# First attention of a two-layer hybrid block: second score pass over 64 rows on alternating halves of the array

## The chip, the cores and the metric

The kernel runs on one core of a Trainium2 chip, as one launch. The metric is device time in microseconds: 2327.08 us is the median of three runs (2325.67 to 2328.69). The profiled execution, from which every duration below comes, took 2329.05 us; its span from the first to the last instruction is 2327.2 us. The engines are named as in the profile: PE (TensorE matmul), PEld (its weight loads), DVE (VectorE), ACT (ScalarE), POOL (GpSimd), SP (SyncE).

## The reference, cut to what matters

Two layers over 512 latent tokens and 256 context tokens, width 1024. Each layer has three token mixers in parallel, then a SwiGLU. The change touches mixer A alone, a grouped-query attention: 8 query heads of 64 channels, 2 key/value heads, queries and keys RMS-normalised per head, latents also rotated.

```python
k_all = jnp.concatenate([kac, ka], axis=1)          # context keys, then latent keys
s = jnp.einsum('bqkgd,bskd->bkgqs', q, k).astype(jnp.float32) * (HEAD_DIM ** -0.5)
p = jax.nn.softmax(s, axis=-1).astype(v.dtype)
return jnp.einsum('bkgqs,bskd->bqkgd', p, v)
```

Latent queries see 512 latent and 256 context keys. Context queries see the 256 context keys; they exist in the first layer only, since the last layer has no context output.

## The kernel before, in words

**Numbers in two parts.** The operands of a matmul have type fp32r, which keeps fewer bits than float32. So an array is held as a high part (the value written as fp32r) and a low part (the value minus the high part), and a product is a sum of partial products.

**Queries and keys of the first attention.** For a pair of heads c, `q_st[0][c][x]` is a tile of 128 partitions by 768 tokens for head 2c+x. Its high part has the 64 partitions of half x, its low part the other half. `k_hh[0]` has a key head's high part on both halves, `k_ll[0]` its low part on both halves. One matmul over all 128 rows with `k_hh` gives (high + low) times high key, a second one with `k_ll` gives (high + low) times low key; both add up in PSUM.

**Work items.** Token tiles of 128: 0 to 3 latents, 4 and 5 context. `ORDER[0]` puts them in pairs, whose first member is side 0 and whose second is side 1: (0,1), (3,2) and, in layer 0 alone, (4,5). An item n is a head and a pair, n = head x pairs + j; layer 0 has 24 items, layer 1 has 16. Side 0's scores lie in PSUM banks 0 and 1, side 1's in banks 2 and 3 (`SCORES_AT`). For a latent tile each pass is two matmuls, 512 latent keys and 256 context keys; for a context tile it is one over 256.

**The order on each engine** is written out by hand. PE, in the loop of `attention` for mixer A, item n: `score(n + 1, 0)`, `score(n + 1, 1)`; `turn(n, 0)`, `turn(n, 1)` (transposes of the probabilities, L2292, four to a group); half of a fill (`fill`, L2340: projection work for the gates, put between the attention's steps); `turn(n, 2)`; now and then a `piece` (L2137: transposes that make the queries or keys of a later pair of heads); `attend(n, groups 0 and 1)` (L2310); the other half of the fill; `attend(n, group 2)`. A context pair has one group instead of three. `score` (L2273) does all of side 0, both passes, and then all of side 1; the last matmul of a side raises `scored`. `turn` and `piece` wait until the transposes two before them have been read by DVE (`lo_out`).

**DVE**, item n: `fold(n - 1)` (L1672, after ACT's `o_half` L958, after the last `attend`); `maximum(n + 1, 0)` and `maximum(n + 1, 1)` (L1645, negated by L1648), each after its `scored`; `turned_lo(n, 0)` (L1662, `pt_lo`), `invert(n + 1, 0)` (L1655), `turned_lo(n, 1)`, `invert(n + 1, 1)`, `turned_lo(n, 2)`, then a piece's low part (L1461). **ACT** does the high part of each turned group (L949), the exponentials (L941), and a piece's high part (L884). **POOL** multiplies the probabilities by the inverse sums (L582).

**Pieces of queries.** For either head of a pair ACT copies 64 rows of PSUM to the head's half of `q_st`, and DVE writes the difference to the other half: two instructions on each engine, 512 columns (latents) or 256 (context). There are 12 such pieces: 4 pairs of heads, latents in both layers, context in the first.

Of the kernel before, what the change touches and what calls it, by code (L numbers as in the profile page):

```python
# [5 lines left out]
F32 = mybir.dt.float32  # L6
F32R = mybir.dt.float32r
I32 = mybir.dt.int32
ALU = mybir.AluOpType
ACT = mybir.ActivationFunctionType  # L10
# [4 lines left out]
LAT, CTX = 512, 256  # L15
P = 128
# [3 lines left out]
TOK = LAT + CTX  # L20
HALF = TOK // 2
HD = 64
# [21 lines left out]
ADA_SLOTS = 3  # L44


ORDER = (((0, 1), (3, 2), (4, 5)), ((0, 1), (2, 3), (4, 5)))

FILLS = 8
KEY_COPIES = 2 * 16  # L50
# [3 lines left out]
SCORES_AT = ((0, 1024), (0, 512))  # L54
# [186 lines left out]
def build(nc, x_in, ctx_in, cond, cond_cols, w_first, w_ada, b_ada, stream, qk_gain, norm_rows, bias, ident_in,  # L241
# [8 lines left out]
    def sb(name, shape, dtype=F32, at=None):  # L250
        size = (2 if dtype == mybir.dt.bfloat16 else 4) * int(np.prod(shape[1:]))
        if at is None:
            at = cursor[0]
            cursor[0] += (size + 63) // 64 * 64
        assert at + size <= end, (name, at + size - end)
        return nc.alloc_sbuf_tensor_at(name, shape, dtype, offset=at)
# [57 lines left out]
    q_st = [[[sb(f"q_st{b}{c}{x}", [P, TOK], F32R, at=R + Q_AT[b][c] * K + 3 * K * x) for x in range(2)]  # L314
             for c in range(KB)] for b in range(2)]
    k_hh = [sb(f"k_hh{b}", [P, (2, 4)[b], TOK], F32R, at=R + (87, 42)[b] * K) for b in range(2)]
    k_ll = [sb(f"k_ll{b}", [P, (2, 4)[b], TOK], F32R, at=R + (93, 54)[b] * K) for b in range(2)]
# [35 lines left out]
    ps = nc.alloc_psum_tensor("ps", [P, 8, 512], F32)  # L353
# [55 lines left out]
    def S(name):  # L409
        if name not in sems:  # L410
            sems[name] = nc.alloc_semaphore(name)
        return sems[name]
# [14 lines left out]
    def at(ph, name):  # L427

        return ph.at.get(name, 0) + (PRIME if name in PRIMED else 0)
# [16 lines left out]
    with block:  # L446
# [116 lines left out]
        def _(pool):  # L563
# [9 lines left out]
            def attention(ph):  # L573
                pairs, branch = ph.tiles // 2, ph.part

                def normalise(n, i):

                    j, c = n % pairs, 2 * (n % 2) + i
                    keys = P * len(key_tiles(branch, ORDER[branch][j][i]))
                    pool.wait_ge(S("inverse"), at(ph, "inverse") + 2 * n + i + 1)  # L580
# [51 lines left out]
        def _(act):  # L632
# [240 lines left out]
            def piece(ph, what, h, part):  # L873

                order = turn_order(ph)[what, h, part]
                a, b = ((0, LAT), (LAT, TOK))[part]
                act.wait_ge(S("turned_p"), at(ph, "turned_p") + order + 1)
                for x in range(2):
                    rows = slice(HD * x, HD * x + HD)
                    if what == "q":  # L880
                        dst, src = q_st[0][h][x][rows, a:b], ps[rows, turn_bank(ph, order), 0:b - a]
                    else:
                        dst, src = k_hh[0][rows, h, a:b], ps[HD * h:HD * h + HD, turn_bank(ph, order), 0:b - a]
                    last = nc.scalar.activation(dst, src, ACT.Copy)  # L884
                last.then_inc(S("hi_out"), 1)

# [42 lines left out]
            def attention(ph):  # L929
# [3 lines left out]
                def probs(n, i):  # L933

                    j, c = n % pairs, 2 * (n % 2) + i
                    keys = P * len(key_tiles(branch, ORDER[branch][j][i]))
                    act.wait_ge(S("max_ready"), at(ph, "max_ready") + 2 * n + i + 1)
# [242 lines left out]
        def _(dve):  # L1180
# [268 lines left out]
            def piece(ph, what, h, part):  # L1449

                order = turn_order(ph)[what, h, part]
                a, b = ((0, LAT), (LAT, TOK))[part]
                dve.wait_ge(S("hi_out"), at(ph, "hi_out") + order + 1)
                for x in range(2):
                    rows, other = slice(HD * x, HD * x + HD), slice(HD * (1 - x), HD * (2 - x))
                    if what == "q":
                        src, dst, hi = rows, q_st[0][h][x][other, a:b], q_st[0][h][x][rows, a:b]
                    else:
                        src = slice(HD * h, HD * h + HD)
                        dst, hi = k_ll[0][rows, h, a:b], k_hh[0][src, h, a:b]  # L1460
                    last = nc.vector.tensor_tensor(dst, ps[src, turn_bank(ph, order), 0:b - a], hi.bitcast(F32), ALU.subtract)  # L1461
                last.then_inc(S("lo_out"), 1)

# [157 lines left out]
            def attention(ph):  # L1621
# [3 lines left out]
                def maximum(n, i):  # L1625

                    h, j = divmod(n, pairs)
                    m, t = 2 * n + i, ORDER[branch][j][i]
                    keys = P * len(key_tiles(branch, t))
# [258 lines left out]
        def _(pe):  # L1888
# [356 lines left out]
            def attention(ph):  # L2245
                pairs, branch, turns = ph.tiles // 2, ph.part, turn_order(ph)
                count = HEADS * pairs

                def score(n, i):

                    h, j = divmod(n, pairs)
                    t, m = ORDER[branch][j][i], 2 * n + i
                    if branch == 0 and i == 0 and h % 2 == 0:
                        if j == 0:
                            pe.wait_ge(S("lo_out"), at(ph, "lo_out") + turns["q", h // 2, 0] + 1)
                            if h % 4 == 0:
                                pe.wait_ge(S("lo_out"), at(ph, "lo_out") + turns["k", h // 4, 1] + 1)
                        elif j == 2:
                            pe.wait_ge(S("lo_out"), at(ph, "lo_out") + turns["q", h // 2, 1] + 1)
                    elif branch == 1 and i == 0 and j == 0 and h % 2 == 0:  # L2260
                        pe.wait_ge(S("fill_lo"), at(ph, "fill_lo") + passes_to(ph, h))
                        pe.wait_ge(S("k_dup"), at(ph, "k_dup") + KEY_COPIES * (h // 2))
                    if n:

                        pe.wait_ge(S("probs"), at(ph, "probs") + m - 1)
                    q, kv = q_st[branch][h // 2][h % 2], h // 4 if branch == 0 else h % 4
                    for part, kk in enumerate((k_hh[branch], k_ll[branch])):
                        lat = latent_keys(branch, t)
                        for keys, first, w in ((lat, 0, P * len(lat)), (None, P * len(lat), CTX)):
                            if not w:  # L2270
                                continue
                            at_col = SCORES_AT[branch][i] + first
                            last = nc.tensor.matmul(ps[:, at_col // 512, at_col % 512:at_col % 512 + w], q[:, t * P:(t + 1) * P],  # L2273
                                                    tile_cols(kk[:, kv, :], keys) if keys else kk[:, kv, LAT:TOK],
                                                    start=part == 0 and at_col % 512 == 0, stop=part == 1, skip_group_check=True)
                    last.then_inc(S("scored"), 1)

                def turn(n, g):
# [6 lines left out]
                    for kt in turn_groups(branch, j)[g]:  # L2285
                        for i, t in sorted(enumerate(ORDER[branch][j]), key=lambda e: e[1]):
                            tiles = key_tiles(branch, t)
# [7 lines left out]
                def attend(n, some):  # L2295
# [3 lines left out]
                    for g in some:  # L2299
# [3 lines left out]
                        for x, kt in enumerate(groups[g]):  # L2303
                            v = v_a[:, kt, h // 4, :] if branch == 0 else v_b[:, h // 2, kt, h % 2, :]
                            users = [t for t in ORDER[branch][j] if kt in key_tiles(branch, t)]
                            w, side = P * len(users), P * (min(users, key=lambda t: t % 2) % 2)
# [222 lines left out]
def latent_keys(branch, t):  # L2529

    if t >= LT:
        return ()
    return NEAR_TILES[t] if branch else tuple(range(LT))


def key_tiles(branch, t):

    return latent_keys(branch, t) + tuple(range(LT, ALLT))
# [7 lines left out]
def turn_groups(branch, j):  # L2546

    if j == 2:
        return ((LT, LT + 1),)
    if branch == 0:  # L2550
        return ((LT, LT + 1), (0, 1), (2, 3))
    return ((LT, LT + 1), ((1, 0, 2), (3, 2, 0))[j])
# [8 lines left out]
def tile_cols(cols, tiles):  # L2561

    return cols[:, 0:LAT].rearrange("p (a b) -> p a b", b=P)[:, tiles[0]:tiles[-1] + 1:tiles[-1] - tiles[0] if len(tiles) == 2 else 1, :]
# [19 lines left out]
    return (((1, 0, 4),), ((5, 0, 3), (0, 3, 1)))[j]  # L2583


def start_pieces(ph):

    if ph.part:
        return []
    return [("k", 0, 0), ("q", 0, 0), ("k", 0, 1)] + [("q", 0, 1)] * (ph.tiles > LT)  # L2590
# [14 lines left out]
def turn_bank(ph, order):  # L2605

    return order if order < len(start_pieces(ph)) else TURN_BANK[ph.part] + order % 2


def turn_order(ph):  # L2610

    pairs = ph.tiles // 2
    names = start_pieces(ph) + slot_pieces(ph, -1)
    for n in range(HEADS * pairs):
        names += [("p", n, g) for g in range(len(turn_groups(ph.part, n % pairs)))]
        names += slot_pieces(ph, n)
    return {name: i for i, name in enumerate(names)}
# [19 lines left out]
def passes_to(ph, f):  # L2637

    return sum(len(fill_passes(ph, n)) for n in range(f))
# [195 lines left out]
```

## Time and profile before

| | us |
|---|---|
| median of three runs | 2327.08 |
| profiled execution | 2329.05 |
| its span | 2327.2 |
| PE busy, 97% of the span | 2254.0 |
| DVE busy, 51% | 1187.5 |
| ACT busy, 40% | 929.6 |
| POOL busy, 47% | 1084.1 |

Busy time of PE is not PE at its peak: a matmul's row contains its way through the array, so that rows overlap. The pitch from one start to the next says what a matmul costs in a stream. An idle gap that a row names is therefore shorter than the time that PE loses. The first attention runs from about 262 to 420 us (layer 0) and from about 1533 to 1658 us (layer 1).

### The profile page before, as it was taken

The numbers are of one execution on the slowest core, as the hardware profiler recorded it, in microseconds if no ns is written. First come the engines' busy times: TensorE is split into PE (matmuls) and PEld (weight loads), VectorE is DVE, ScalarE is ACT, GpSimd is POOL, SyncE is SP. The second block draws the span as 40 slices with busy tenths as digits, with TensorE's granted clock in tenths as the row PEclk, the third lists the DMA queues.
The fourth block names the chain that finished last, engine by engine and source line by source line (L and its number), as shares of the span: only waits on it lengthen the run. The fifth ranks groups of instructions, "written<-read, shape, count | busy, mean of one in ns | idle before, by whom it ended". The sixth has DMA issues, their size and how long they took to land.

```text
span 2327.2 us, 34375 instructions
## 1 busy us (share of the span) xinstructions
PE 2254.0 (97%) x13050; PEld 2072.4 (89%) x13050; DVE 1187.5 (51%) x2429; ACT 929.6 (40%) x1854; POOL 1084.1 (47%) x852
## 2 busy tenths in 40 slices
PE   7999999999999999999999989999999999999997
PEld 4899988989999999999999878888889899888887
DVE  5979766527632546654831173656637426212114
ACT  4232466436622651111111254256546447322223
POOL 1334445435534553433533443455545567545545
PEclk9999999999999999999999999999999999999999
DMA  6634200122114445443522433221223256333345
GB/s 267 216 117 131 96 27 24 60 71 82 58 63 136 159 156 187 135 151 117 163 84 66 158 130 128 64 64 37 64 84 98 80 185 189 118 99 100 109 122 176
DMA packets 120083, 266.00 MB, mean 114 GB/s; under 512 B 13701, under 2 KB 13957, under 8 KB 118537
## 3 DMA queue, kind: packets, MB, share of 16 engines
q1 hardware_dynamic: 109728, 238.08, 31.7%
q10 hardware_dynamic: 10216, 26.09, 3.3%
q8 instruction: 85, 1.39, 0.2%
q14 instruction: 54, 0.43, 0.1%
HBM read 250.48 MB, written 10.49 MB: 112 GB/s over the span
## 4 chain that ended last, share of the span: by engine, by line
PE 85%; DVE 8%; ACT 3%; issue 1%; DMA 1%; POOL 1%; ACTq 0%; SPq 0%; DVEq 0%
PE ps L1932 31%; PE ps L1934 13%; PE ps L1944 13%; PE ps L2340 8%; PE ps L2045 7%; PE ps L2310 4%; PE ps L2292 3%; PE ps L2273 2%; PE ps L2119 1%; DVE pt_lo L1662 1%; DVE max_c L1645 1%; DVE ada_unused_gate_up L1192 1%; ACT p_sb L941 1%; DMA raw<-in_stream 1%; PE ps L2000 1%
## 5 line engine op out<-in xcount | busy, mean ns | idle before, releaser
L570 POOL TENSOR_TENSOR w_lo<-raw,w_hi 128x512 fp32r<-128x512 f32 x632 | 864.5, 1390 | 963.8 <-ACT w_hi L648 963.1
L648 ACT ACTIVATE w_hi<-raw 128x512 fp32r<-128x512 f32 x632 | 367.5, 627 | 671.1 <-PE ps L1934 247.1
L1932 PE MATMUL ps<-h_hi,w_lo 128*128 128x384 f32 (+1 forms) x832 | 301.1, 362 | 0.0
L1932 PE MATMUL ps<-h_hi,w_hi 128*128 128x384 f32 (+1 forms) x832 | 300.4, 361 | 0.0
L1932 PE MATMUL ps<-h_lo,w_hi 128*128 128x384 f32 (+1 forms) x832 | 300.4, 361 | 0.0
L582 POOL TENSOR_TENSOR p_sb<-p_sb,row_inv 128x768 f32<-128x768 f32 (+1 forms) x160 | 178.9, 1126 | 197.5 <-DVE row_inv L1655 196.1
L1759 DVE TENSOR_TENSOR ps<-silu_g,ps 128x768 f32<-128x768 f32 (+3 forms) x52 | 37.7, 726 | 377.3 <-PE ps L1934 177.8
L1932 PEld LDWEIGHTS ps<-h_hi,w_lo 128*128 128x128 f32 x832 | 156.2, 188 | 15.8
L1932 PEld LDWEIGHTS ps<-h_lo,w_hi 128*128 128x128 f32 x832 | 156.2, 188 | 15.8
L1932 PEld LDWEIGHTS ps<-h_hi,w_hi 128*128 128x128 f32 x832 | 156.2, 188 | 15.8
L2340 PE MATMUL ps<-h_hi,w_lo 128*128 128x384 f32 (+1 forms) x408 | 147.9, 362 | 3.0 <-DVE v_b L1610 2.3
L1192 DVE SCALAR_TENSOR_TENSOR ada_unused_gate_up<-ada_raw_gate_up,ada_cond_gate_up 128x1024 bf16<-128x1024 f32 x96 | 143.0, 1490 | 5.2 <-DMA ada_raw_gate_up<-in_w_ada 0.2
L2340 PE MATMUL ps<-h_lo,w_hi 128*128 128x384 f32 (+1 forms) x408 | 144.4, 354 | 0.0
L2340 PE MATMUL ps<-h_hi,w_hi 128*128 128x384 f32 (+1 forms) x408 | 144.2, 353 | 0.0
L1934 PE MATMUL ps<-h_hi,w_hi 128*128 128x384 f32 x424 | 141.6, 334 | 0.0
L1934 PE MATMUL ps<-h_hi,w_lo 128*128 128x384 f32 x424 | 141.6, 334 | 0.0
L1934 PE MATMUL ps<-h_lo,w_hi 128*128 128x384 f32 x424 | 141.6, 334 | 0.0
L941 ACT ACTIVATE p_sb<-ps,neg_max 128x768 f32<-128x768 f32 (+1 forms) x160 | 117.0, 731 | 45.6 <-DVE neg_max L1642 36.7
L1662 DVE TENSOR_TENSOR pt_lo<-ps,pt_hi 128x512 fp32r<-128x512 f32 x176 | 118.2, 687 | 30.8 <-ACT pt_hi L949 29.5
L949 ACT ACTIVATE pt_hi<-ps 128x512 fp32r<-128x512 f32 x176 | 101.8, 598 | 63.1 <-PE ps L2292 62.0
L1164 ACT ACTIVATE silu_g<-ps 128x768 f32<-128x768 f32 (+1 forms) x36 | 25.4, 706 | 209.1 <-PE ps L1934 130.5
L2292 PE MATMUL ps<-ident,p_sb 128*128 128x128 f32 x704 | 96.7, 275 | 2.0 <-DVE pt_lo L1662 1.0
(246 smaller groups left out, 5503.4 us busy)
## 6 DMA issues: line engine op xcount, KB each, us to landing
raw<-in_stream SPq DMA_DIRECT2D x632, 256.0 KB, 2.8
ada_raw_gate_up<-in_w_ada SPq DMA_DIRECT2D x48, 512.0 KB, 3.6
ada_raw_tokens_a<-in_w_ada SPq DMA_DIRECT2D x16, 512.0 KB, 3.7
ada_raw_merge_c<-in_w_ada SPq DMA_DIRECT2D x16, 512.0 KB, 3.8
bias_sb<-in_bias ACTq DMA_DIRECT2D x32, 256.0 KB, 2.6
scratch<-xr ACTq DMA_DIRECT2D x16, 512.0 KB, 4.3
xr<-scratch SPq DMA_DIRECT2D x14, 512.0 KB, 4.3
first_raw<-in_w_first SPq DMA_DIRECT2D x5, 1024.0 KB, 14.2
```

The lines of the kernel that those rows point to most:

```text
L570: nc.gpsimd.tensor_tensor(w_lo[:, u % 2, cols], raw[:, u % 2, cols], w_hi[:, u % 2, cols].bitcast(F32), ALU.subtract).then_inc(S("lo_made" ...
L582: nc.gpsimd.tensor_tensor(p, p, row_inv[:, c:c + 1].broadcast_to([P, keys]), ALU.mult).then_inc(S("p_ready"), 1)
L648: nc.scalar.activation(w_hi[:, s, cols], raw[:, s, cols], ACT.Copy).then_inc(S("hi_made"), 1)
L941: nc.scalar.activation(p_sb[branch][n % 2][i][:, 0:keys], region(branch, i, 0, keys), ACT.Exp, bias=neg_max[:, i:i + 1], accum_out=row_sum ...
L1192: nc.vector.scalar_tensor_tensor(ada_unused[kind][:, :], ada_raw[kind][:, u % ADA_SLOTS, :], 1.0, ada_cond[kind][:, c, :], ALU.mult, ALU.m ...
L1662: nc.vector.tensor_tensor(pt_lo[branch][:, a:a + w], ps[:, turn_bank(ph, order), 0:w], pt_hi[branch][:, a:a + w].bitcast(F32), ALU.subtrac ...
L1932: last = nc.tensor.matmul(bank(0), tile, x[:, k, 0:split], start=start, stop=stop)
L1934: last = nc.tensor.matmul(bank(1), tile, x[:, k, HALF:TOK], start=start, stop=stop)
L1944: last = nc.tensor.matmul(ps[:, bank, 0:b - a], w[:, s, k * P:(k + 1) * P], x[:, k, a:b], start=k == 0 and name == TERMS[0], stop=k == k_t ...
L2045: last = nc.tensor.matmul(ps[:, banks[t], 0:cols], x[:, k, t * P:(t + 1) * P], w[:, s, kk * cols:(kk + 1) * cols], start=k == 0 and name = ...
L2292: last = nc.tensor.transpose(ps[:, turn_bank(ph, order), col:col + P], p_sb[branch][n % 2][i][:, a:a + P], ident[:, :])
L2340: last = nc.tensor.matmul(ps[:, bank, 0:b - a], w[:, u % 2, k * P:(k + 1) * P], x[:, k, a:b], start=r == 0, stop=r == FILL_STEPS - 1, skip ...
```

## The change

The first pass stays as it is, over 128 rows with `k_hh`, side 0 and then side 1. The second pass multiplies the high part of the queries alone with `k_ll`, over the 64 rows on which that high part lies; the product of the two low parts is left out. Its matmuls come after both sides' first pass, in the order latent keys of side 0, of side 1, context keys of side 0, of side 1. For this, side 1 has its high part on the half opposite to side 0: the queries are written by tile, even tiles to half x and odd tiles to the other, which takes four instructions a piece on ACT and on DVE where there were two, each with half the columns. The second latent pair becomes (2,3), so that side and parity of the tile agree. `scored` of side 0 is raised by the third matmul of the second pass.

```diff
-ORDER = (((0, 1), (3, 2), (4, 5)), ((0, 1), (2, 3), (4, 5)))
+ORDER = (((0, 1), (2, 3), (4, 5)),) * 2
@@ ACT piece
                     if what == "q":
-                        dst, src = q_st[0][h][x][rows, a:b], ps[rows, turn_bank(ph, order), 0:b - a]
+                        for side in range(2):
+                            last = nc.scalar.activation(side_cols(q_st[0][h][x][half_rows(x + side), a:b], side),
+                                                        side_cols(ps[rows, turn_bank(ph, order), 0:b - a], side), ACT.Copy)
+                        continue
@@ DVE piece
                     if what == "q":
-                        src, dst, hi = rows, q_st[0][h][x][other, a:b], q_st[0][h][x][rows, a:b]
+                        for side in range(2):
+                            last = nc.vector.tensor_tensor(side_cols(q_st[0][h][x][half_rows(x + side + 1), a:b], side),
+                                                           side_cols(ps[rows, turn_bank(ph, order), 0:b - a], side),
+                                                           side_cols(q_st[0][h][x][half_rows(x + side), a:b].bitcast(F32), side), ALU.subtract)
+                        continue
@@ PE attention
+                def scores_of(n, side, rows, kk, parts=(True, False), done=False):
+                    h, j = divmod(n, pairs)
+                    t = ORDER[0][j][side]
+                    lat = latent_keys(0, t)
+                    for latents in parts:
+                        if latents and not lat:
+                            continue
+                        a, b = (0, LAT) if latents else (LAT, TOK)
+                        col = SCORES_AT[0][side] + (0 if latents or not lat else LAT)
+                        last = nc.tensor.matmul(ps[:, col // 512, col % 512:col % 512 + b - a], q_st[0][h // 2][h % 2][rows, t * P:(t + 1) * P],
+                                                kk[rows, h // 4, a:b], start=kk is k_hh[0], stop=kk is k_ll[0], skip_group_check=True)
+                    if done:
+                        last.then_inc(S("scored"), 1)
@@ score(n, i)
+                    if branch == 0:
+                        if i == 0:
+                            for side in range(2):
+                                if n:
+                                    pe.wait_ge(S("probs"), at(ph, "probs") + m + side - 1)
+                                scores_of(n, side, slice(0, P), k_hh[0])
+                            return
+                        for latents in range(2):
+                            for side in range(2):
+                                scores_of(n, side, half_rows(h + side), k_ll[0], (latents == 0,), latents == 1)
+                        return
+def half_rows(x):
+    return slice(HD * (x % 2), HD * (x % 2) + HD)
+def side_cols(cols, side):
+    return cols.rearrange("p (a b) -> p a b", b=P)[:, side::2, :]
```

## Rows read from the trace of the kernel before

**Rows 1.** The page: busy time of each engine, share of the span, instructions.

```profile
PE 2254.0 (97%) x13050; PEld 2072.4 (89%) x13050; DVE 1187.5 (51%) x2429; ACT 929.6 (40%) x1854; POOL 1084.1 (47%) x852
```

**Rows 2.** Timeline, 1586.5:1594.3, one item: start us, us, engine, line [idle before].

```profile
1586.91 0.52 PE L2273 MATMUL ps<-k_hh,q_st 128*128 128x512 f32 x2
...
1587.52 0.42 DVE L1672 TENSOR_TENSOR o_sum<-ps,o_half 64x256 f32<-64x256 f32 x1 [0.61 <-ACT o_half L958]
...
1587.86 0.94 DVE L1645 TENSOR_REDUCE max_c<-ps 128x1 f32<-128x768 f32 x1
...
1589.96 0.68 DVE L1662 TENSOR_TENSOR pt_lo<-ps,pt_hi 128x512 fp32r<-128x512 f32 x1
...
1590.35 0.40 PE L2340 MATMUL ps<-h_hi,w_hi 128*128 128x512 f32 x1
...
1590.70 0.66 PE L2292 MATMUL ps<-ident,p_sb 128*128 128x128 f32 x4
...
1590.95 0.69 DVE L1662 TENSOR_TENSOR pt_lo<-ps,pt_hi 128x512 fp32r<-128x512 f32 x1 [0.24 <-ACT pt_hi L949]
...
1592.28 0.40 PE L2340 MATMUL ps<-h_hi,w_lo 128*128 128x512 f32 x1
...
1594.14 0.40 PE L2273 MATMUL ps<-k_hh,q_st 128*128 128x512 f32 x1
```

**Rows 3.** Chain that ended last, in 1586:1602: start us, us, engine and line.

```profile
1595.21 0.97 DVE max_c L1645
...
1597.41 0.61 DVE pt_lo L1662
...
1598.06 0.66 PE ps L2292 x4
```

**Rows 4.** Timeline, 325:332, layer 0, item 8, whose probabilities are a context pair's.

```profile
325.22 0.52 PE L2273 MATMUL ps<-k_hh,q_st 128*128 128x512 f32 x2
...
326.17 0.94 DVE L1645 TENSOR_REDUCE max_c<-ps 128x1 f32<-128x768 f32 x1
...
328.30 0.34 PE L2340 MATMUL ps<-h_hi,w_hi 128*128 128x384 f32 x1
...
329.10 0.36 PE L2310 MATMUL ps<-pt_lo,v_a 128*128 128x256 f32 x1 [0.46 <-DVE pt_lo L1662]
...
331.96 0.96 DVE L1645 TENSOR_REDUCE max_c<-ps 128x1 f32<-128x768 f32 x1 [1.06 <-PE ps L2273]
```

**Rows 5.** Timeline, 1547.4:1553: an item of layer 1 that has a piece.

```profile
1547.51 0.52 PE L2273 MATMUL ps<-k_hh,q_st 128*128 128x512 f32 x2
...
1552.30 0.65 PE L2137 MATMUL ps<-ident,tok_a 128*128 128x128 f32 x4 [0.35 <-DVE pt_lo L1662]
```

**Rows 6.** Timeline, around 353: the first transposes of an item wait for POOL.

```profile
353.43 1.10 PE L2292 MATMUL ps<-ident,p_sb 128*128 128x128 f32 x8 [0.15 <-POOL p_sb L582]
```

**Rows 7.** Second score pass, layers 0 and 1: count, ns min/median/max, starts, forms.

```profile
L2273 PE MATMUL ps<-k_ll,q_st x80: 274/283/392, 263.0 to 418.9; 128*128 128x256 f32 x48, 128*128 128x512 f32 x32
...
L2273 PE MATMUL ps<-k_ll,q_st x64: 278/340/403, 1533.8 to 1646.9; 128*128 128x512 f32 x32, 128*128 128x256 f32 x32
```

**Rows 8.** Timeline of weight loads, 520:523, six starts (four loads between these left out).

```profile
520.47 0.19 PEld L2310 LDWEIGHTS ps<-pt_lo,v_b 128*128 128x128 f32 x1
...
521.03 0.19 PEld L2310 LDWEIGHTS ps<-pt_hi,v_b 128*128 128x128 f32 x1
```

**Rows 9.** Timeline, 340:352: the first two matmuls of a fill behind transposes.

```profile
340.41 0.42 PE L2340 MATMUL ps<-h_hi,w_lo 128*128 128x384 f32 x1
340.67 0.34 PE L2340 MATMUL ps<-h_lo,w_hi 128*128 128x384 f32 x1
```

**Rows 10.** Instructions of query pieces on ACT and DVE: count, ns min/median/max.

```profile
L884 ACT ACTIVATE q_st<-ps x24: 366/592/600, 256.0 to 1607.5; 64x512 fp32r<-64x512 f32 x16, 64x256 fp32r<-64x256 f32 x8
...
L1461 DVE TENSOR_TENSOR q_st<-ps,q_st x24: 417/683/694, 257.3 to 1608.9; 64x512 fp32r<-64x512 f32 x16, 64x256 fp32r<-64x256 f32 x8
```

**Rows 11.** Timeline, layer 1: the load for the first score matmul.

```profile
1533.30 0.30 PEld L2273 LDWEIGHTS ps<-k_hh,q_st 128*128 128x128 f32 x2 [0.30 <-DVE k_ll L1461]
```

More of the change, by code:

```diff
@@ L880, in piece @@
                     if what == "q":
-                        dst, src = q_st[0][h][x][rows, a:b], ps[rows, turn_bank(ph, order), 0:b - a]
-                    else:
-                        dst, src = k_hh[0][rows, h, a:b], ps[HD * h:HD * h + HD, turn_bank(ph, order), 0:b - a]
+                        for side in range(2):
+                            last = nc.scalar.activation(side_cols(q_st[0][h][x][half_rows(x + side), a:b], side),
+                                                        side_cols(ps[rows, turn_bank(ph, order), 0:b - a], side), ACT.Copy)
+                        continue
+                    dst, src = k_hh[0][rows, h, a:b], ps[HD * h:HD * h + HD, turn_bank(ph, order), 0:b - a]
                     last = nc.scalar.activation(dst, src, ACT.Copy)
@@ L1454, in piece @@
                 for x in range(2):
-                    rows, other = slice(HD * x, HD * x + HD), slice(HD * (1 - x), HD * (2 - x))
+                    rows = slice(HD * x, HD * x + HD)
                     if what == "q":
-                        src, dst, hi = rows, q_st[0][h][x][other, a:b], q_st[0][h][x][rows, a:b]
-                    else:
-                        src = slice(HD * h, HD * h + HD)
-                        dst, hi = k_ll[0][rows, h, a:b], k_hh[0][src, h, a:b]
+                        for side in range(2):
[3 more added lines that the diff above has]
+                        continue
+                    src = slice(HD * h, HD * h + HD)
+                    dst, hi = k_ll[0][rows, h, a:b], k_hh[0][src, h, a:b]
                     last = nc.vector.tensor_tensor(dst, ps[src, turn_bank(ph, order), 0:b - a], hi.bitcast(F32), ALU.subtract)
```

## The prediction

> **What bounds the kernel now.** The page first: PE is busy 97% of the span, no other engine more than 51% [rows 1]. That speaks for PE, so that every matmul saved should count. But the page is an average over stages, and the change lies in one of them. So next the timeline of one item of the first attention. I count from T, the start of its score block (1586.91), and write times as T+x.
>
> PE gives scores for T to T+1.41, then eight transposes and six fill matmuls, the last of which starts at 1590.35 = T+3.44 [rows 2]. With about 0.23 of pitch PE is free at T+3.67, but the third group of transposes starts at T+3.79 (1590.70). It is the one that waits for DVE: DVE folds at T+0.61, takes the first maximum at T+0.95, the second at T+2.00, and the low part of group 0 from T+3.05 to T+3.73 [rows 2]. These follow each other without a gap. With M for the start of the first maximum the transposes start at M+2.84. The chain of waits says the same of the next item (T = 1594.14): maximum at T+1.07, low part, transposes at T+3.92 = M+2.85, with DVE on the path [rows 3]. So here the order of DVE, not PE, sets the time from T to the third group, by 0.1 to 0.25 us. The slack comes back in part: the low part of group 1 (from 1590.95 to 1591.64, T+4.73) holds PE too, and the second half of the fill starts at T+5.37 [rows 2]; from transposes without such a wait it is 1.46 behind them (T+3.92 leads to T+5.38 next door). So the second fill starts at max(T+5.37, M+4.30).
>
> Other kinds of item. Where a context pair's probabilities are worked on (7 in layer 0), PE has one group of transposes, starts its last fill matmul at T+3.08 and waits for the same low part to T+3.88 [rows 4]; that is M+2.93 with M = 0.95. Where a piece is made (5 in layer 1), the piece's transposes wait for group 1's low part to T+4.79 [rows 5]. Where POOL is late (3 in layer 0) its probabilities decide [rows 6]. Where the scores made are a context pair's (8), PE itself is the bound within 0.05 to 0.1 us.
>
> What holds M? In most items the fold (M = 0.95 or 1.07). With no fold ahead, the first maximum starts at 331.96 against T = 331.07, straight from the scores: side 0's scores can be read at T+0.89 [rows 4]. So the slack between scores and the maximum is only 0.06 to 0.18 us.
>
> **The second pass.** It has 64 matmuls of 512 columns and 80 of 256 in both layers [rows 7]. A side of a latent pair takes 1.41/2 = 0.70 for two passes, so 512 and 256 columns together take 0.35, of which some 0.23 and 0.12. If the 64-row matmuls of the two sides run beside each other, each pair of them costs as much as one; if they don't, nothing is saved. The trace has no 64-row matmul; the bounds are 0 and 0.35 us for a latent pair, 0.12 for a context pair. Weight loads limit it: six successive loads start 0.11 apart [rows 8] where matmuls are short, and the pass needs four. So 0.45 instead of 0.69, a saving of 0.24 on PE's own time, and none for a context pair. I take this value, since the halves share neither array rows nor PSUM banks; the other end stays as a rival. The Trainium skill, "TensorE: Matmul & The Clock Gate", Part 3 (Packing small matmuls), says that matmuls on different row groups run at once, 3.07 times as fast for four of 32 rows; no run here shows it yet.
>
> **What it does to `scored`.** Before, side 0 was ready after its own two passes, at 0.70 of matmul time. Now both first passes (0.70) and three matmuls of the second come first: latent of side 0 (0.23) and context of side 0 (0.12), with side 1's beside them. Side 0 becomes readable 0.345 later, at T+1.24. Without overlap side 1's 0.23 is added: 0.57 later, T+1.46. Side 1 is ready before DVE gets to it in either case.
>
> **Change of mode.** The pass goes from 128 rows to 64 and back. Nothing like it is in the trace. Nearest is the change from transposes to fp32r matmuls, whose first matmul lasts 0.42 instead of 0.34 and has its successor 0.26 behind it [rows 9]: 0.085 a change. Bounds: nothing, and 0.28, if a matmul must leave the array (0.28 of duration less 0.12 of pitch) and a load of 0.11 is then exposed. I take 0.085, each way. The first change delays `scored`: M = 1.32. The Trainium skill, "TensorEngine Tiling (Array Packing)", Tiling Modes, holds that changing the tiling mode drains TensorE; by that rule the cost would lie near my upper end.
>
> **The sum**, with M = 1.32:
> - Layer 1, 9 items without a piece: second fill at 5.62 instead of 5.37, +0.245: 2.2.
> - Layer 1, 5 with a piece: low part of group 1 ends at M+3.50, piece at 4.87 instead of 4.80: 0.35. The fifteenth has enough filler.
> - Layer 0, scores of the second pair: 3 items at +0.28, 2 with a piece at +0.10, 3 behind POOL at 0: 1.0.
> - Layer 0, context pair's probabilities: wait ends at M+2.93 = 4.25 instead of 3.88 (4 items) or 4.02 (3): 4 x 0.37 + 3 x 0.23 = 2.2.
> - Scores of a context pair: two changes of mode, 0.17 less 0.02, on PE's path; 8 x 0.15, less 0.09 in four: 0.85.
> - The blocks where DVE isn't waited for (first of each layer, last of layer 1): 0.17 less 0.24 each: -0.2.
> - Query pieces: four instructions of 0.37 on ACT for two of 0.59, four of 0.42 on DVE for two of 0.68 [rows 10]: +0.3 on each. It is hidden by PE's second fill inside the attention (DVE's next work is the fold), but ahead of layer 1's first scores DVE is waited for [rows 11]: +0.3. Without cover, 12 x 0.3 = 3.6.
> - The order (2,3) for (3,2) changes no count and no wait, since the transposes wait for both sides: 0.
>
> Together +6.7 us. Against the profiled 2329.05 that makes 2335.8; the median of the runs shown lies 1.97 lower, so 2333.8. PE's saving of 32 x 0.24 = 7.7 vanishes since PE arrives earlier at waits that end later.
>
> **Rivals.**
> - Overlap with no cost of the mode: M = 1.24; by the same list +1.4, 0, +0.6, +1.6, -0.2, -0.7, +0.3 = +3.1: 2330.2.
> - No overlap, no cost of the mode: M = 1.46; +3.5 and +1.05 in layer 1, +1.8 and +3.15 in layer 0, +0.3: +9.8, 2336.9. For it speaks that nothing in the trace shows overlap; the matmuls would then keep their pitch of 0.23. This is also the case where the change does not do what it says.
> - No overlap and 0.085 a change: M = 1.55: +13.6, 2340.7. Overlap with a full drain (0.28): M = 1.52 and 8 x 0.5 on PE: +16, 2343.
> - Faster: overlap holds and DVE's chain does not pass the delay on. The place is the fold and the first maximum: if side 0's readiness at T+1.24 fell within the time DVE is held anyway, PE would keep 0.24 in the 32 latent blocks less the cost of the mode, 4 to 8 us: 2319 to 2323. It decides where M stays at 1.07 or below; the fold ends at T+1.03 at the latest and no DVE work stands behind it, which speaks against it.
>
> **Chances and range.** My case 35% (2333.8, own range 2331.5 to 2336); overlap without cost 20%; no overlap without cost 18%; the dearer ones together 9%; faster 10%; the remaining 8% for a smaller loss, part of it made good elsewhere (POOL's and ACT's order), within +3. The range is 2328 to 2340.5. What a measurement can tell from no change is 0.2%, 4.65 us: slower by more has my case nearly whole, no overlap and the dearer ones: 0.60; within 0.2% has overlap without cost and the small losses: 0.30; faster 0.10.
>
> **What would show it.** Second-pass starts of the two sides: about 0.11 apart (overlap, load bound), or 0.23 (none). The gap from the last `k_hh` matmul to the first of 64 rows beyond its pitch: the cost of the mode. The first L1645 at T+1.32 instead of T+0.95; the third group of transposes at T+4.16 instead of T+3.79; the context pair's L2310 at T+4.25; longer idle time of PE put down to DVE `pt_lo` L1662. The prediction fails if M does not move, or if the third group starts before M+2.84.

## The result and the profile after

The changed kernel took 2340.36 us (median of four runs, 2338.39 to 2341.12), the one before 2326.38 beside it. The medians are 13.98 us apart. The ratio of the two kernels on record is 1.0049, 95% interval 1.0037 to 1.0060: slower by some 11.4 us, between 8.6 and 14.0, so that the gap of these medians is at the upper end. The text below reckons with 11.4; the spans of the two profiled executions are 12.1 apart. The forecast was slower by 6.7, at 2333.8. The direction and the mechanism held; the size was too small. The measured median lies 0.14 us inside the upper end of the stated range (2340.5) and well outside the range given for the case itself (2331.5 to 2336).

The page of the changed kernel, span and busy time:

```profile
span 2339.3 us, 34423 instructions
...
PE 2258.5 (97%) x13050; PEld 2061.3 (88%) x13050; DVE 1192.2 (51%) x2453; ACT 937.6 (40%) x1878; POOL 1084.6 (46%) x852
```

PE has the same number of instructions and 4.5 us more of busy time, not less, against [rows 1]. The page says nothing more. The group of score matmuls does (count, ns min/median/max, first and last start, forms; then what the engine waited for, us and times):

```profile
L2264 PE MATMUL ps<-k_hh,q_st x144: 274/283/502, 261.0 to 1656.6; 128*128 128x256 f32 x80, 128*128 128x512 f32 x64
L2264 PEld LDWEIGHTS ps<-k_ll,q_st x144: 182/183/187, 261.9 to 1656.9; 64*128 64x128 f32 x144
L2264 PE MATMUL ps<-k_ll,q_st x144: 271/382/502, 261.9 to 1657.2; 64*128 64x256 f32 x80, 64*128 64x512 f32 x64
...
  issue: 8.0, 32
```

The forms are those of [rows 7], now with 64 rows. The 8.0 us "issue" (time in which the engine waited for nothing that the profile shows), 32 times, stand ahead of loads: 0.25 us before each latent block's 64-row pass. Before, the same group had 0.4 us of it, once.

One item of layer 1 without a piece, the partner of [rows 2] (start us, us, engine, line; idle time in brackets). T = 1594.48:

```profile
1594.48 0.87 PE L2264 MATMUL ps<-k_hh,q_st 128*128 128x512 f32 x4
...
1595.20 0.42 DVE L1677 TENSOR_TENSOR o_sum<-ps,o_half 64x256 f32<-64x256 f32 x1
1595.28 0.30 PEld L2264 LDWEIGHTS ps<-k_ll,q_st 64*128 64x128 f32 x4 [0.26 <-issue]
1595.28 0.62 PE L2264 MATMUL ps<-k_ll,q_st 64*128 64x512 f32 x4
...
1595.83 1.09 PE L2323 MATMUL ps<-ident,p_sb 128*128 128x128 f32 x8
1595.93 0.96 DVE L1650 TENSOR_REDUCE max_c<-ps 128x1 f32<-128x768 f32 x1 [0.31 <-PE ps L2264]
...
1596.68 0.48 PE L2371 MATMUL ps<-h_hi,w_lo 128*128 128x512 f32 x1
...
1598.05 0.68 DVE L1667 TENSOR_TENSOR pt_lo<-ps,pt_hi 128x512 fp32r<-128x512 f32 x1
...
1598.78 0.66 PE L2323 MATMUL ps<-ident,p_sb 128*128 128x128 f32 x4 [0.46 <-DVE pt_lo L1667]
...
1600.23 0.40 PE L2371 MATMUL ps<-h_hi,w_lo 128*128 128x512 f32 x1
```

Side by side with the item of before:

| event, us after T | before | forecast | changed |
|---|---|---|---|
| 64-row pass starts | (second pass, side after side) | 0.78 | 0.80 |
| first transposes | 1.41 | about 1.3 | 1.35 |
| first maximum (M) | 0.95 | 1.32 | 1.45 |
| fill starts | 2.20 | | 2.20 |
| third group of transposes | 3.79 | 4.16 | 4.30 |
| second fill | 5.37 | 5.62 | 5.75 |
| next item | 7.23 | 7.48 | 7.61 |

In the old kernel DVE reached the maximum from the fold. Now it waits 0.31 us for the scores, and this wait is the row to look for. The four 64-row matmuls do overlap: from the first of them to the transposes is 0.55 us, where four such matmuls take 0.70 before, and the single records of the trace have the two sides' matmuls start 0.004 us apart, neither the 0.11 nor the 0.23 of the forecast's signs. Yet the fill starts at T+2.20 in both kernels: in a latent block PE gains nothing at all. The chain of waits, 1594:1603, now runs through both maxima, as it does in every such item:

```profile
1594.64 1.30 PE ps L2264 x8
1595.94 0.96 DVE max_c L1650
...
1597.08 0.88 DVE max_c L1650
...
1598.13 0.61 DVE pt_lo L1667
...
1598.78 0.66 PE ps L2323 x4
```

In layer 0, item 8, the context pair's probabilities, the partner of [rows 4] with T = 326.18:

```profile
327.62 0.96 DVE L1650 TENSOR_REDUCE max_c<-ps 128x1 f32<-128x768 f32 x1 [0.41 <-PE ps L2264]
...
330.56 0.36 PE L2341 MATMUL ps<-pt_lo,v_a 128*128 128x256 f32 x1 [0.99 <-DVE pt_lo L1667]
```

M is 1.44, the low part reaches PE at T+4.38 instead of T+3.88, and PE's idle time in front of it grew from 0.46 to 0.99. From the second score block to the last, layer 0's items took 153.83 us instead of 147.99 and layer 1's 109.62 instead of 105.35: +10.1 of the 11.4. Layer 1's tail, from the last score block to the merge's matmuls behind it, adds 0.5 (15.77 for 15.31). Ahead of layer 1's first scores the load waits 0.92 us where [rows 11] have 0.30, which adds 0.6:

```profile
1539.40 0.65 PEld L2264 LDWEIGHTS ps<-k_hh,q_st 128*128 128x128 f32 x4 [0.92 <-DVE k_ll L1466]
```

### The profile page after: what moved, and what is told of

It is laid out like the page before. It is cut to its first block, busy times and chain, and to the rows that moved or that the text cites. A ratio compares the mean times of both kernels' runs of the same rounds, so it can differ in the third digit from the quotient of the medians.

```text
span 2339.3 us, 34423 instructions
## 1 busy us (share of the span) xinstructions
PE 2258.5 (97%) x13050; PEld 2061.3 (88%) x13050; DVE 1192.2 (51%) x2453; ACT 937.6 (40%) x1878; POOL 1084.6 (46%) x852
## 4 chain that ended last, share of the span: by engine, by line
PE 83%; DVE 10%; ACT 3%; issue 1%; DMA 1%; POOL 1%; ACTq 0%; SPq 0%; DVEq 0%
PE ps L1937 30%; PE ps L1939 13%; PE ps L1949 12%; PE ps L2371 7%; PE ps L2050 7%; PE ps L2341 4%; PE ps L2323 2%; DVE max_c L1650 2%; PE ps L2264 2%; PE ps L2124 1%; PE ps L2304 1%; DVE pt_lo L1667 1%; DMA raw<-in_stream 1%; DVE ada_unused_gate_up L1194 1%; DVE ada_unused_merge_c L1194 1%
```

## The experiments

Three theories stood at the start. D: side 0's scores are ready later, and DVE's order hands that on to PE. M: what costs is PE's own change between 128 and 64 rows. P: the longer query pieces delay DVE and ACT.

**The order alone, over 128 rows.**

```diff
-scores_of(n, side, half_rows(h + side), k_ll[0], (latents == 0,), latents == 1)
+scores_of(n, side, slice(0, P), k_ll[0], (latents == 0,), latents == 1)
```

> Queries, order of the matmuls and place of scored as in the changed kernel, but the second pass over all 128 rows (it then adds the product of the low parts again): no overlap and no change of mode. Theory D (what costs is that side 0's scores are ready later, passed on by DVE's order): without overlap side 0 is ready 0.57 us after its old time, so the first maximum starts at T+1.46, where the changed kernel has 1.44; third group of transposes at T+4.3, items of layer 1 at 7.6 instead of 7.23; in all +9 to +12 us, nearly all of the changed kernel's loss, although PE does the work of before. Theory M (what costs is PE's change between 128 and 64 rows): this kernel has none, so within 1.5 us of before. The context pair's score blocks must fall back to a pitch of 0.47 in either theory.

Measured: 1.0049, interval 1.0036 to 1.0063, the loss of the changed kernel, without a single 64-row matmul. Its score block, T = 1576.62:

```profile
1576.62 0.88 PE L2264 MATMUL ps<-k_hh,q_st 128*128 128x512 f32 x4
...
1577.33 0.86 PE L2264 MATMUL ps<-k_ll,q_st 128*128 128x512 f32 x4
...
1578.03 1.04 PE L2323 MATMUL ps<-ident,p_sb 128*128 128x128 f32 x8
1578.11 0.96 DVE L1650 TENSOR_REDUCE max_c<-ps 128x1 f32<-128x768 f32 x1 [0.45 <-PE ps L2264]
```

PE's block is 1.41 as before, the first maximum starts at T+1.49, the item takes 7.66. PE does exactly the old work and the kernel is as slow as the changed one. That the change of mode alone costs, theory M, falls; D stands. The run does not say that the mode is free in the changed kernel. It takes away two things there, the change of mode ahead of side 0's scores (0.19 us, next experiment) and the overlap (0.23), which nearly cancel: T+1.49 against T+1.45. In the changed kernel the order makes side 0 late by 0.345 and the change of mode by 0.19 more, and DVE hands on both. By the forecast's formula T+1.24 would leave +0.17 in a plain item of layer 1, where +0.38 was measured; so some half of the loss there goes back to the mode. This is an estimate: no run has the overlap without the mode.

**The 64-row pass, side after side.**

```diff
-scores_of(n, side, slice(0, P), k_hh[0])                      # both sides, then the interleaved second pass
+scores_of(n, i, slice(0, P), k_hh[0])                         # one side
+scores_of(n, i, half_rows(h + i), k_ll[0], done=True)
```

> The 64-row second pass, but each side's right behind its own first pass, so that sides never overlap and the mode changes four times a block instead of twice. Theory D: side 0 is ready at 0.89 plus one entry into the 64-row mode (0.20 in the changed kernel's trace), first maximum at T+1.09; now PE itself is late, its block takes 1.41 + 2 x 0.20 + 2 x 0.10 = 2.0 and the context pair's 0.47 + 0.6; items of layer 1 +0.5 to +0.6, in all +15 to +20 us. If an entry is dear only because side 1's matmul waits for side 0's (a load conflict) and not for the mode, the entry here costs under 0.1 and the kernel stays within +5 us.

Measured: 1.0115 (1.0099 to 1.0130), +26.8 us, more than the 15 to 20 expected. T = 1588.59:

```profile
1588.59 0.51 PE L2264 MATMUL ps<-k_hh,q_st 128*128 128x512 f32 x2
...
1589.03 0.61 PE L2264 MATMUL ps<-k_ll,q_st 64*128 64x512 f32 x2
...
1589.58 0.62 PE L2264 MATMUL ps<-k_hh,q_st 128*128 128x512 f32 x2
1589.68 0.96 DVE L1650 TENSOR_REDUCE max_c<-ps 128x1 f32<-128x768 f32 x1
...
1590.12 0.61 PE L2264 MATMUL ps<-k_ll,q_st 64*128 64x512 f32 x2
...
1590.67 1.09 PE L2318 MATMUL ps<-ident,p_sb 128*128 128x128 f32 x8
```

The first maximum is at T+1.09 as computed, and the block takes 2.08. From 128 rows to 64 rows the next start is 0.44 behind instead of 0.35. The 64-row pair then takes 0.55 instead of 0.35: 0.1 in its first matmul, and 0.1 on leaving. The second 128-row pair takes 0.54, which holds the gap ahead of the next entry and 0.1 more in its own first matmul. So either change costs some 0.19 us, 0.09 of gap and 0.10 in the first matmul behind it; where the eight transposes follow, the second part is 0.06. What the estimate lacked is this second part of leaving: it had 0.10 for it and so a block of 2.0. PE is now late by itself: the block is 0.66 longer, the transposes take 0.06 more, and the plain item grows by just that, 7.95 for 7.23. Group 1's low part comes late with it (T+4.78 instead of T+4.04).

**The pieces alone.** Tiles in turn on either half, four instructions a piece, pair (2,3); the matmuls of before.

```diff
+scores_of(n, i, slice(0, P), k_hh[0])
+scores_of(n, i, slice(0, P), k_ll[0], done=True)
```

> Queries written by tile in four instructions a piece and the pair (2,3), as in the changed kernel, with the matmuls of before (128 rows in both passes, side after side). Theory D: the pieces lie beside PE's second fill inside the attention and cost only ahead of the first scores: first maximum back at T+0.95 to 1.07, +0.3 to +1 us in all. Theory P (the longer pieces delay DVE and ACT, and so the items with a piece): 12 x 0.3 = +3.6 us or more, seen in items with a piece alone.

Measured: 0.9999 (0.9990 to 1.0008). T = 1594.24: M is 1.07, as in [rows 3], and the items add up to 148.43 and 105.39. P falls; with the orders of before, this part of the change is free within 2 us. The load ahead of layer 1's first scores does wait 0.91 us here too, against 0.30 before, so these 0.6 belong to the pieces.

```profile
1594.24 0.51 PE L2264 MATMUL ps<-k_hh,q_st 128*128 128x512 f32 x2
...
1595.31 0.96 DVE L1650 TENSOR_REDUCE max_c<-ps 128x1 f32<-128x768 f32 x1
```

**Both sides on the same half**, so that the 64-row matmuls can't run beside each other.

```diff
-q_st[0][h][x][half_rows(x + side), a:b]      and  scores_of(n, side, half_rows(h + side), ...)
+q_st[0][h][x][half_rows(x), a:b]             and  scores_of(n, side, half_rows(h), ...)
```

> As the changed kernel, but both sides' high parts lie on the same half, so that the four 64-row matmuls use the same rows and can't run beside each other; order, mode changes, four-instruction pieces and scored stay. Theory D with full overlap in the changed kernel: side 0's scores come another 0.23 us later, first maximum at T+1.44+0.23 = T+1.67, third group at T+4.53, context pair's block 0.12 longer (0.76); 26 x 0.2 + 8 x 0.1 = 5 to 6 us more than the changed kernel, +18 to +21 in all. If in the changed kernel the latent pair's matmuls don't really overlap (both have a duration of 0.495 there, instead of 0.39), this kernel gives the same as the changed one within 2 us.

Measured: 1.0076 (1.0062 to 1.0089), +17.7 us, just under the 18 to 21 expected. T = 1579.89:

```profile
1580.69 0.96 PE L2264 MATMUL ps<-k_ll,q_st 64*128 64x512 f32 x4
1581.57 0.96 DVE L1650 TENSOR_REDUCE max_c<-ps 128x1 f32<-128x768 f32 x1 [0.65 <-PE ps L2264]
...
1581.58 1.09 PE L2323 MATMUL ps<-ident,p_sb 128*128 128x128 f32 x8
```

The second pass takes 0.89 us to the transposes instead of 0.55, and M is 1.68 instead of 1.45. The overlap in the changed kernel is thus whole: it is worth 0.23 + 0.11, one matmul of each width. It saves 6.3 us against this kernel and still doesn't pay for the modes and the order.

**DVE out of the way.** On DVE the low parts of groups 0 and 1 come ahead of the maximum of side 1, on ACT their high parts ahead of the exponential of side 0, in the changed kernel and in the one before. The two orders, DVE's left and ACT's right (written out; an item of three groups):

```diff
 # DVE                                        # ACT
 maximum(n + 1, 0)                            turned_hi(n, 0)
-maximum(n + 1, 1)                            +turned_hi(n, 1)
 turned_lo(n, 0)                              probs(n + 1, 0)
-invert(n + 1, 0)                             -turned_hi(n, 1)
 turned_lo(n, 1)                              +turned_hi(n, 2)
+invert(n + 1, 0); maximum(n + 1, 1)          probs(n + 1, 1)
-invert(n + 1, 1)                             -turned_hi(n, 2)
 turned_lo(n, 2)
+invert(n + 1, 1)
```

> The changed kernel with DVE's and ACT's order in the first attention turned so that PE's transposes no longer wait behind both maxima: DVE does maximum of side 0, low parts of groups 0 and 1, then the maximum of side 1; ACT does the high parts of groups 0 and 1 before the exponential of side 0, and that of group 2 before the exponential of side 1. No instruction is added or taken away. Theory D: the third group of transposes then starts when PE is free, at T+3.6 instead of T+4.3; items of layer 1 at about 6.9 instead of 7.61; layer 0's less, since there POOL's normalising of the context pair's items comes next; in all 8 to 16 us less than the changed kernel, so +0 to +6 or below against before. Theory M (PE's own change of mode, which stays): at most 2 us less than the changed kernel, items of layer 1 at 7.6.

> The kernel before with the same turned orders on DVE and ACT. It too waited for DVE, by 0.1 to 0.25 us in the items with three groups. Theory D: third group at T+3.67, items of layer 1 at about 6.97 instead of 7.23, those with a piece at 7.4 instead of 8.1; in all -3 to -9 us. With DVE out of the way only PE's own time is left between this kernel and the changed one with these orders: 0.07 saved in each of 32 blocks, 0.18 lost in each of 8, 0.3 lost at the pieces ahead of the first scores: the two within 2.5 us of each other, where the plain ones are 14 apart. If they stay 8 or more apart, the loss isn't in DVE's chain.

Measured: the changed kernel with these orders 1.0016 (1.0007 to 1.0025), the one before with them 0.9998 (0.9989 to 1.0007). The loss fell from 11.4 us to 3.7 without a matmul touched, and the two kernels lie 4.2 apart instead of 11.4. That is more than the 2.5 foreseen, but half of the 8 that would have spoken against D. The gain of 7.7 in the changed kernel is just short of the 8 to 16 expected. A plain item of layer 1, first of the changed kernel (T = 1626.34), then of the one before (T = 1622.43):

```profile
1627.79 0.96 DVE L1649 TENSOR_REDUCE max_c<-ps 128x1 f32<-128x768 f32 x1 [0.20 <-PE ps L2266]
...
1629.01 1.29 DVE L1666 TENSOR_TENSOR pt_lo<-ps,pt_hi 128x512 fp32r<-128x512 f32 x2
...
1630.01 0.60 PE L2325 MATMUL ps<-ident,p_sb 128*128 128x128 f32 x4
...
1633.26 0.40 PE L2266 MATMUL ps<-k_hh,q_st 128*128 128x512 f32 x1
```

```profile
1623.73 0.96 DVE L1644 TENSOR_REDUCE max_c<-ps 128x1 f32<-128x768 f32 x1
...
1625.11 1.29 DVE L1661 TENSOR_TENSOR pt_lo<-ps,pt_hi 128x512 fp32r<-128x512 f32 x2 [0.24 <-ACT pt_hi L949]
...
1626.11 0.60 PE L2294 MATMUL ps<-ident,p_sb 128*128 128x128 f32 x4
...
1629.35 0.40 PE L2275 MATMUL ps<-k_hh,q_st 128*128 128x512 f32 x1
```

Third group at T+3.67 and T+3.68, item 6.92 and 6.92: with PE as the bound, the 64-row pass is worth nothing. M still differs (T+1.45 against T+1.30) and no longer matters.

So the 4.2 between the two kernels must lie elsewhere, and the traces have it in the pieces. Three items of layer 1 and three of layer 0, each behind a piece, take 0.66 to 0.71 us more in the changed kernel (together 4.1); all others agree within 0.06. Such an item, first of the changed kernel (T = 1589.99), then of the one before (T = 1587.43):

```profile
1590.38 1.73 DVE L1459 TENSOR_TENSOR q_st<-ps,q_st 64x256 fp32r<-64x256 f32 x4 [1.28 <-ACT q_st L882]
...
1592.47 0.94 DVE L1649 TENSOR_REDUCE max_c<-ps 128x1 f32<-128x768 f32 x1
```

```profile
1587.46 1.39 DVE L1460 TENSOR_TENSOR q_st<-ps,q_st 64x512 fp32r<-64x512 f32 x2 [0.92 <-ACT q_st L884]
...
1589.22 0.94 DVE L1644 TENSOR_REDUCE max_c<-ps 128x1 f32<-128x768 f32 x1
```

DVE ends the piece's low part 0.7 us later, as it starts 0.36 later behind ACT's copies and lasts 0.34 longer, and the fold and the maximum (T+2.48 for T+1.79) stand behind it. The four instructions a piece, free with the old orders, are not free with these. No run has the turned orders with pieces of two instructions and the 64-row pass, so this is read from the rows and not tested.

The expected -3 to -9 of the kernel before did not come: layer 1's items gained 6.0 (99.35 us), but layer 0's took 150.06 instead of 147.99, since POOL normalises later there and the first transposes of some items wait for it to T+2.6 (T+1.70 before), and layer 1's tail lost 1.3 in the same way. (The tail of this profile is 1.4 longer still, in a stretch from 1653 to 1657 us with a granted clock of 0.54 to 0.61, which no other profile has there.)

**The context pair's second pass over 128 rows**, in the changed kernel with the turned orders.

```diff
-scores_of(n, side, half_rows(h + side), ...)
+scores_of(n, side, half_rows(h + side) if j < 2 else slice(0, P), ...)
```

> As the changed kernel with the turned orders, but the context pair's second pass over 128 rows, where 64 rows only cost a change of mode. Theory D: context pair's score block 0.47 instead of 0.64, 8 x 0.17 = 1.4 us less than with 64 rows where PE is the bound there, less where POOL is; 0 to 1.5 us below the changed kernel with the turned orders.

Measured: 1.0017 (1.0008 to 1.0026), no difference that can be told from the 1.0016 without it. The context blocks do get shorter, but the transposes behind them start where they did, at T+0.69 to T+0.71 or T+1.11 to T+1.15, now waiting for POOL's probabilities.

**The turned orders where they help**, in layer 1, all but the last two items (a condition in front of the same lines), in either kernel.

> The kernel before with the turned orders on DVE and ACT in layer 1 alone, up to the last item but two; layer 0, where POOL's normalising became late under them, and the last items keep theirs. In the trace of the kernel before with turned orders everywhere, layer 1's items from the second to the last took 99.35 us instead of 105.35, layer 0's 2.1 more and layer 1's tail 1.3 more. Theory D: -4 to -6 us, 0.9975 to 0.998 of before. If the gain of layer 1 is given back after the attention, within 2 us of before.

> The changed kernel with the same orders in layer 1 alone. Items of layer 1 without a piece at 6.92 instead of 7.61, 101.4 instead of 109.6 from the second to the last; layer 0 unchanged at +5.8 and the tail at +0.6: 7 to 8 us less than the changed kernel, +5 to +7 against before, and so 9 to 12 above the kernel before with these orders, of which most is layer 0's DVE chain.

Measured: the kernel before with them 0.9974 (0.9965 to 0.9983), 6 us faster than before and so the fastest of all; its layer 1 items take 99.37 us and layer 0's 148.07. The changed kernel with them 1.0006 (0.9997 to 1.0015): 10 us less than without, more than the 7 to 8 expected (its items of layer 1 say 8.2), and 7.5 above the former, less than the 9 to 12 expected. In layer 0 its items remain at 153.83, 5.8 above the former. What else separates the two are three items of layer 1 behind a piece, 0.66 each for the reason above (7.57 instead of 6.91 in two of them).

## Why the prediction was right in sign and short in size

- **DVE's order, not PE, sets the time from T to the third group**: right. Third group at M+2.85 in the changed kernel, at M+2.86 with the order alone, M+2.84 in the forecast. The context pair's wait ended at M+2.94 (forecast M+2.93).
- **Order of the matmuls, +0.345 to `scored`**: right. The order alone, without overlap, gives M = 1.48 to 1.49 (forecast 1.46).
- **Overlap**: right that it is there, and the value of 0.45 for the pass happened to be right for a wrong reason, which was luck. Loads do not limit it: the four 64-row loads start at 1595.278, .281, .386 and .389, so that the two of a pair start together and the pairs 0.105 apart, all within 0.11 us, where four at the pitch of [rows 8] need 0.33. The streams take 0.23 + 0.12 and the other 0.1 is in the first matmul, which starts with its load and lasts that much longer; the 0.09 to the transposes comes on top. For the context pair the forecast had 0.02 for the overlap, and it gives 0.12.
- **Change of mode, 0.085 taken, bounds 0 and 0.28**: this is the term that was mis-sized. An entry measures 0.19 (0.09 of gap and 0.10 in the first matmul), an exit 0.15 ahead of transposes and 0.19 ahead of a 512-column matmul. The row I drew on, fp32r matmuls behind transposes [rows 9], shows the longer first matmul only and not the gap ahead of it. The Trainium skill's sentence that a change of tiling mode drains TensorE ("TensorEngine Tiling (Array Packing)", Tiling Modes) was taken as a cost near the upper end, 0.28. The trace puts the entry at 0.19, about midway between that and 0.085, and does not show whether it is a drain.
- **The sum.** With M = 1.44 instead of 1.32 the items of the list grow as measured: 9 x 0.38 and 5 x 0.17 in layer 1 (together 4.3, forecast 2.55), 3 x 0.38 and 2 x 0.19 at the second pair's scores and 0 behind POOL (1.5, forecast 1.0), 4 x 0.5 and 3 x 0.37 at the context pair's probabilities (3.2, forecast 2.2), and 0.06 to 0.23 in the seven context blocks that lie within these items (1.1, forecast 0.85 for eight). That is the 10.1 of the trace.
- **PE's saving vanishes**: right, and more so. I gave PE 0.24 less two changes, 0.07 a block. The overlap gives 0.35 and the two changes take 0.34 (0.19 and 0.09 up to the transposes, and 0.06 in them, 0.85 instead of 0.79), so that 0 is left at the fill's start.
- **Pieces hidden inside the attention**: right, as long as the orders are those of before. The 0.3 ahead of layer 1's first scores is 0.6 in the rows (the load waits 0.92 for 0.30), too little to be told in the ratio.
- **The rival "faster"** named the right condition, M at or below 1.07. M did move, and so it fell. "No overlap, no cost of the mode" had the right order of magnitude (+9.8) for the wrong kernel: that one is the experiment with the order alone, +11.4. Nearest in number was "no overlap and 0.085 a change" (2340.7), whose mechanism the run on the same half rules out for the changed kernel. The list of the rival "overlap with no cost" adds up to +3.0, not the +3.1 written there.

Items, tail and the wait ahead of layer 1's scores make 11.2 of the 11.4 us. Of the 4.2 us between the two kernels with turned orders everywhere the traces show 4.1: 2.05 in layer 1 (101.40 against 99.35) and 2.1 in layer 0 (152.15 against 150.06), in the items behind a piece. What stays open is what the change of mode and the order cost each by itself in the changed kernel, and whether pieces of two instructions would give back these 4.1.

## What to carry to other kernels

Before you interleave the work of two results to let it overlap, ask who waits for the first of them: here the consumer had 0.06 to 0.18 us of slack, the interleaving took 0.345 and the change of mode 0.19 more, and the rest went to the total in 26 items, though PE is "97% busy" and got no slower in the latent blocks. A saving on the busiest engine counts only from the point at which that engine is the last to arrive. When a chain through a lesser engine holds the busy one, look at the order of that engine's own instructions first: moving one maximum behind two subtractions, and ACT's exponentials with it, gave 6 us in layer 1, where the 64-row pass gave nothing even with DVE out of the way. And a part that is free in one order (the pieces of four instructions) need not be free in the next.

## What the runs showed of the hardware

- Matmuls over 64 rows on opposite halves, into different PSUM banks, ran fully beside each other: a pass of 2 x 512 and 2 x 256 columns took 0.34 us less (0.55 for 0.89) than the same on one half.
- Going from 128 rows to 64 cost 0.19 us, 0.09 of it a gap and 0.10 in the first matmul. Going back cost 0.19 ahead of a 512-column matmul and 0.15 ahead of transposes. A context pair's block of 0.47 became 0.65, although the second pass' columns ran in half the time.
- Loads of 64-row weights have the duration of 128-row ones (183 ns against 188). Two on opposite halves start together (0.003 us apart); on the same half the first two are 0.108 apart.
